# Grouping the three products of a split-precision accumulation by pass instead of by contraction tile

## What is computed

```python
u = rmsnorm(h, norm_g[0])
proj = u @ w_in                      # hc, bc, cc, q, k, v, gates
y_conv = (bc * conv3(cc * hc)) @ w_conv_out
o = diff_attention(q1, q2, k1, k2, vh, lam)        # 4 heads, ALiBi bias
y_attn = (rmsnorm(o, subln_g) * (1 - lam_init)) @ w_attn_out
m = (g0 * y_conv + g1 * y_attn) @ w_o
h = h + rmsnorm(m, norm_g[1])
u = rmsnorm(h, norm_g[2])
f = jnp.square(jax.nn.relu(u @ w_ff1)) @ w_ff2     # 1024 -> 4096 -> 1024
h = h + rmsnorm(f, norm_g[3])
```

## Time and profile before

| | |
|---|---|
| time, median of 3 runs | 1601.73 us (1598.68 to 1604.53) |
| span of the profiled execution | 1602.1 us (its own time is not given beside it) |
| TensorE, matmuls / weight loads | 1540.1 us busy (96%) / 1244.7 us (78%), 6,989 each |
| VectorE, ScalarE, POOL | 50%, 31%, 7% busy |
| mean granted TensorE clock | 0.986 of full |
| transfers | 105.60 MB moved, 66 GB/s over the span |

### The profile page before, as it was taken

How to read it: one execution, slowest core, us unless ns; L and a number is a source line. 1 busy time by engine, 2 the same in 40 slices (tenths; PEclk the granted TensorE clock), 3 DMA queues, 4 the chain that set the end, 5 groups by cost and what they waited for, 6 DMA issues and landing times.

```text
span 1602.1 us, 18405 instructions
## 1 busy us (share of the span) xinstructions
PE 1540.1 (96%) x6989; PEld 1244.7 (78%) x6989; DVE 793.8 (50%) x1160; ACT 493.0 (31%) x683; POOL 108.3 (7%) x67
## 2 busy tenths in 40 slices
PE   5999999999999999999989999999999999999996
PEld 4877877777778777888868788888888888888785
DVE  6387486576666532664667323333233333333464
ACT  5334344344434542012334322121302121121242
POOL 0000000000000000002442420000000000000032
PEclk9999999999999999999999999999999999999997
DMA  4111102011101123436211221111111111111312
GB/s 155 47 44 49 40 27 66 27 38 52 40 26 59 59 90 120 145 121 195 76 55 64 79 79 53 39 52 50 41 52 39 52 52 39 52 52 53 92 53 105
DMA packets 142692, 105.60 MB, mean 66 GB/s; under 512 B 3709, under 2 KB 130874, under 8 KB 142650
## 3 DMA queue, kind: packets, MB, share of 16 engines
q1 hardware_dynamic: 137216, 94.38, 19.4%
q10 hardware_dynamic: 4858, 8.55, 1.4%
q0 software_dynamic: 576, 2.10, 0.3%
HBM read 92.44 MB, written 12.58 MB: 66 GB/s over the span
## 4 chain that ended last, share of the span: by engine, by line
PE 83%; DVE 8%; issue 4%; ACT 3%; POOL 1%; DMA 0%; ACTq 0%; POOLq 0%; SPq 0%; DVEq 0%
PE psum L549 77%; PE psum L619 2%; PE psum L692 1%; PE psum L604 1%; DVE staging L1310 1%; DVE m L1310 1%; DVE act_lo L1075 1%; PE psum L608 1%; POOL m L527 1%; DVE acc L1310 1%; ACT e L922 1%; DVE act_lo L1076 0%; ACT w_hi L835 0%; DMA xn<-in_x 0%; ACT at_hi L927 0%
## 5 line engine op out<-in xcount | busy, mean ns | idle before, releaser
L549 PE MATMUL psum<-act_hi,w_hi 128*128 128x512 f32 x1280 | 513.3, 401 | 16.3 <-DVE act_lo L1075 6.3
L549 PE MATMUL psum<-act_hi,w_lo 128*128 128x512 f32 x1280 | 502.1, 392 | 0.0
L549 PE MATMUL psum<-act_lo,w_hi 128*128 128x512 f32 x1280 | 501.6, 392 | 0.0
L549 PEld LDWEIGHTS psum<-act_hi,w_hi 128*128 128x128 f32 x1280 | 242.6, 190 | 72.7 <-issue 15.9
L549 PEld LDWEIGHTS psum<-act_hi,w_lo 128*128 128x128 f32 x1280 | 242.2, 189 | 51.9
L549 PEld LDWEIGHTS psum<-act_lo,w_hi 128*128 128x128 f32 x1280 | 242.8, 190 | 50.3 <-issue 2.2
L835 ACT ACTIVATE w_hi<-w_raw 128x1024 fp32r<-128x1024 f32 x144 | 151.7, 1054 | 379.4 <-PE psum L549 369.5
L549 PE MATMUL psum<-f_hi,w_hi 128*128 128x512 f32 x512 | 205.7, 402 | 0.9 <-DVE f_lo L1075 0.9
L549 PE MATMUL psum<-f_hi,w_lo 128*128 128x512 f32 x512 | 202.9, 396 | 0.0
L549 PE MATMUL psum<-f_lo,w_hi 128*128 128x512 f32 x512 | 202.9, 396 | 0.0
L1082 DVE TENSOR_TENSOR w_lo<-w_raw,w_hi 128x1024 fp32r<-128x1024 f32 x120 | 150.1, 1250 | 97.6 <-ACT w_hi L835 96.1
(11 more groups left out here) (145 smaller groups left out, 1420.7 us busy)
## 6 DMA issues: line engine op xcount, KB each, us to landing
w_raw<-in_w_ff SPq DMA_DIRECT2D x80, 512.0 KB
w_raw<-in_w_in SPq DMA_DIRECT2D x40, 512.0 KB
gates_scratch<-staging ACTq DMA_DIRECT2D x32, 256.0 KB, 2.0
gate_in<-gates_scratch SPq DMA_DIRECT2D x16, 512.0 KB, 4.2
w_raw<-in_w_o SPq DMA_DIRECT2D x16, 512.0 KB
xn<-in_x SPq DMA_DIRECT2D x8, 512.0 KB, 8.7
x<-in_x SPq DMA_DIRECT2D x8, 512.0 KB, 4.6
w_raw<-in_w_conv_out SPq DMA_DIRECT2D x8, 256.0 KB
```

What stands on the lines that cost most here:

```text
L549: mm = nc.tensor.matmul(bank, stat(a, kt), moving(b, kt), start=(t == 0), stop=(t == len(terms) - 1))
```

## The change

In `product`, the list of terms now runs over the contraction tiles within each pass, instead of over the passes within each tile. The place of the wait `last` is given anew, so that it still stands ahead of the first use of the last contraction tile. The rule for the square sums is word for word the same: one behind each term of the last pass.

```diff
                 sums = list(between)
                 per_kt = -(-len(sums) // (len(kts) - 1))
-                terms = [(kt, a, b) for kt in kts for a, b in PASSES]
+                terms = [(kt, a, b) for a, b in PASSES for kt in kts]
                 for t, (kt, a, b) in enumerate(terms):
-                    if last and t == len(terms) - len(PASSES):
+                    if last and t == len(kts) - 1:
                         pe.wait_ge(*last)
                     mm = nc.tensor.matmul(bank, stat(a, kt), moving(b, kt), start=(t == 0),
                                           stop=(t == len(terms) - 1))
                     if (a, b) == PASSES[-1]:
                         for _ in range(min(per_kt, len(sums))):
                             square_sum(sums.pop(0))
```

## The result

The changed kernel takes 1614.69 us (median of 5 runs, 1609.48 to 1618.27) against 1603.45 us before (5 runs, 1598.68 to 1606.08). The medians lie 11.2 us apart; the ratio on record is 1.0076, with a 95% interval from 1.0054 to 1.0098, which is 12.2 us (8.7 to 15.7), and the text goes by the ratio from here on. The forecast was 1607.5 us, 5.8 over its starting point, with a range to 1614. The direction was right, the size about half of what came, and the median lies 0.7 us beyond the range.

A forecast was written before the change was run, and what follows sets the result against it. The kernel was taken as bound by TensorE's matmul stream plus its waits. Stalls 3.5 us and clock falls 3 us, 6.5 together, added to 1601.73 less 0.7 for swallowed stalls, gave 1607.5 us; range 1602.5 to 1614.

The forecast's parts named there:

- The pace: Whole matmul stream, steps of 0.227 and 0.233 us: a permuted matmul costs the same, taken as 0.
- both rivals on the pace: Faster: successive tiles take the faster pace, 1595.7 us, chance 0.06; slower: pace falls, up to 1634 us, chance 0.04.
- The moved wait in the open: First chunk h=1 and last chunk h=0, k=0: f_lo wait before term 3 instead of 9, +1.40 us each.
- 3.5 us forecast for all stalls: Moved waits and norm chains without the clock: 1.40 + 1.40 + 0.6 + 0.1 us.
- First chunk, h=0: Unit k=0 stalls 1.96 us for f_lo, delaying sums and spread; net +0.6 us, between 0 and 0.8.
- The norm chains: From last square sum to spread matmul (line 725): cover lost in three places, net 0, +0.6 and 0 us.
- two stops of 0.62: TensorE stops 0.62 us before the spread in W units h=0 and last chunk h=1; net 0 each.
- What was said to be hidden: Last chunk, h=1: 0.62 us at the spread, hidden by 2.1 us of waiting for POOL's m, counted 0.
- The f_lo waits: Sign of being right: TensorE's waits for f_lo grow from 0.9 us in two to over 5 in four.
- The clock: Groups of late, dense square sums: more than half bring a clock fall, about two count at 1.5 us, +3 us.
- The rule on gaps: Skill's rule that clock falls come from waiting gaps, so sums cost nothing; rival without added falls 1605.2 us, chance 0.27.

The follow-up runs named there:

- both placements restored: Changed kernel with square sums back behind terms 2, 5, 8, 11 and the last tile's products held, wait before term 9; against the kernel before: ratio 1.0003.
- wait alone: Kernel before, by tile, sums in old places, only the wait for the last f tile moved from term 9 to term 3: ratio 1.0026, 4.2 us over before.
- late but spaced: Changed kernel with each unit's last square sum left late but the earlier ones three terms apart: ratio 1.0038, 6.1 us over the kernel before.
- sums alone: Kernel before, by tile, wait before term 9, only the square sums moved behind terms 16 to 19 (8 to 10 in short units): ratio 1.0046, 7.4 us over.
- four kernels with dense sums: Changed kernel 1.0076; old order with sums late 1.0046; changed kernel with last tile held back 1.0047; change with two unused 32-byte tensors 1.0016; all against before.

## Why the prediction was right and wrong

- *The pace* (taken as 0): right. The run with both placements restored is at 1.0003, and both rivals on the pace fall. The difference between 0.227 and 0.233 that bounded them goes, by the likeliest reading, with the start of the moving operand, which the change doesn't touch.
- *The moved wait in the open*, 1.40 each: right. The fourth matmul starts 922.89 - 920.19 = 2.70 us into its unit, as written, and the lag grew by 1.31 over that stretch. The wait alone came to 4.2 us, with an interval that holds the 3.5 us forecast for all stalls. What was not seen is that such a stall can bring a half-speed stretch behind it.
- *First chunk, h=0*: the stall was right (866.81 - 864.01 = 2.80, against 0.79 for the three steps, so 2.0 lost; 1.96 was written). Its net, +0.6, came out at -0.44 in the profile: +2.3 by the stall and the spread's wait, -1.2 at the wait for w_lo, and -1.5 by a half-speed stretch that this execution of the kernel before had there and that of the changed kernel had not. Without that stretch it would be +1.1; that the net came out below zero is luck of these two executions.
- *The norm chains*: one stop more in the list of line 725, 0.9 us, in the first chunk, h=0 (877.32). The two stops of 0.62 in the W units and the last chunk did not show in the changed kernel, whose four matmuls ahead of the spread ran at half clock and so covered the chain; they show where the clock held, in the late but spaced run (four stops, 3.3 us). That run is 1.9 us slower than the one with the wait alone, but their intervals overlap. What was said to be hidden was: from the last chunk's spread to the end nothing is lost (10.85 to 10.9), and POOL's m wait went from 2.1 to 1.0.
- *The f_lo waits*: over 5 us, but in three units, not four. The fourth lies behind the half-speed stretch of the last chunk; where no such stretch came (wait alone, late but spaced) there are four.
- *The clock*: this is the step that failed: "the rest leave about two, at 1.5 us: +3 us". The mechanism was right and the term too small. All four groups of four sums had a fall. The two first of a place lasted 6.8 us, not 3.4, and the sum inside them took 1.70 us instead of 0.95. And the later waits hid less than was reckoned: in the profile the four cost 10.0 us, of which two waits took back 0.7 and 1.1, so about 8 net; by the late but spaced run against the changed kernel (1.0076 against 1.0038) density costs 6.1 us, where 3 were forecast. By the run of the sums alone, late in the old order, the term with its norm chains is 7.4 us. In both long stretches the fourth sum of the group fell into the slow time. So it is in the profiles of all four kernels with dense sums: of their 14 falls, the five in which sums of the group still ran for 0.8 us or more at half clock lasted 6.8 us, and the nine that began as the group ended lasted 3.4. That the late sum is why they lasted longer fits all 14; no run tested it by itself. The price was taken from a row of one short fall with dense wide matmuls behind it.
- *The rule on gaps*: the Trainium skill (TensorE: Matmul & The Clock Gate, HAM oscillation — how this bites in real kernels) lays the fall to waiting. The trace agrees with that in and behind the 6.3 us wait for act_lo: from 824.5 to 831.3 before and from 829.2 to 836.0 after, the granted clock is 0.50. But the windows of the changed kernel show a fall behind 3.40 busy of 3.40 us too, twice. Narrow matmuls did not keep the clock up.

The sum of the parts closes within their intervals: wait alone 4.2, sums alone 7.4, together 11.6 us against 12.2 measured for the change. The forecast also took off 0.7 us for stalls that a later wait may swallow, for which no row was given; the later waits took back 0.7 and 1.1 us of the clock's cost in the profile.

## What to carry to other kernels

An edit of the order inside an accumulation was free by itself here, but everything hung into that order by a count (a wait, side work "behind each term of the last pass") moves with it; list those first and price each. Side work of narrow matmuls on TensorE wants wide ones between: in the units of 24 matmuls here three between two blocks held the clock and one did not. In the short units three did not always hold it. And where two groups of equal matmuls run at two paces, compare where their operands start.

## What the runs showed of the hardware

- Matmuls whose moving operand of 128 x 512 words (`fp32r`) starts 32 bytes beyond a multiple of 64, by the kernel's tensor sizes, stepped 0.233 us; at a multiple of 64, 0.227. Two unused 32-byte tensors gave 10.4 us of 1603. That the start of the moving operand is the cause is the likeliest reading, not isolated.
- The granted clock fell to 1.2 GHz behind stretches in which TensorE was busy throughout, with eight-matmul blocks one column wide and one wide product between two of them. In units of 24 matmuls with three between, it held (1.00 over 24 us); in the short units of the first chunk, with three between and short waits beside, it fell in five of eight profiles.
- At the lower clock a block of sums took 1.70 us instead of 0.95. A fall lasted 3.4 us, or 6.8 where sums of the group still ran in it (five of 14).
- Of ten stalls of 1.8 us in five profiles, three had a stretch at half clock behind them; in the one measured, 1.5 us came with it.
- Such stretches come and go between executions of the same kernel, and the scatter goes with them. In the largest set of the kernel before, 24 runs, the eleven with a mean granted clock of 0.988 to 0.990 took 1598.19 to 1601.48 us, the thirteen with 0.985 or 0.986 took 1602.93 to 1606.75.
